# Modulation sums taken as rows in four column tiles, with a small turn in the next body, in place of four products with the sums stationary

## What is computed

```python
mod = c_act @ mod_w[i] + mod_b[i]
sh1, sc1, g1, sh2, sc2, g2, sh3, sc3, g3 = jnp.split(mod, 3 * N_SUB, axis=-1)
h = modulate(rmsnorm(x, norm_g[i, 0]), sh1, sc1)
x = x + FFN_RES * g1[:, None, :] * swiglu(h, ffn_w13[i, 0], ffn_w2[i, 0])
```

## Time and profile before

| | us |
|---|---|
| median of 3 runs | 1813.01 |
| lowest and highest run | 1812.73, 1813.53 |
| span of the profiled execution | 1812.3 |
| PE busy | 1725.8 (95%) |
| DVE busy | 1234.9 (68%) |
| ACT busy | 901.6 (50%) |
| L354 matmuls with 64 columns, 256 records | 32.4 |

### The profile page before, as it was taken

The page is one execution under the profiler, slowest core; times in us unless marked ns, Lnnn a source line. Parts: engine busy times, 40 slices in busy tenths (PEclk is TensorE's granted clock), DMA queues, the critical chain, the costliest instruction groups (busy, mean ns, idle before and its releaser), DMA issues.

```text
span 1812.3 us, 33012 instructions
## 1 busy us (share of the span) xinstructions
PE 1725.8 (95%) x12130; PEld 1582.9 (87%) x12130; DVE 1234.9 (68%) x2056; ACT 901.6 (50%) x1475; POOL 74.9 (4%) x119
## 2 busy tenths in 40 slices
PE   6999999899999999999999999999999999999998
PEld 5899989888999889998778999899877789889997
DVE  6877878668777877766556555689687465455554
ACT  2444457644444434445665444545377755554443
POOL 2000011200000100000001000100000000000000
PEclk9999999999999999999999999999999999999999
DMA  9898857758888698864434655354532155436551
GB/s 352 301 308 296 288 141 203 158 209 265 304 291 289 166 345 284 297 183 138 128 83 114 216 187 189 107 177 149 158 99 71 48 186 170 133 122 196 183 185 67
DMA packets 123657, 352.78 MB, mean 195 GB/s; under 512 B 9850, under 2 KB 52874, under 8 KB 114224
## 3 DMA queue, kind: packets, MB, share of 16 engines
q1 hardware_dynamic: 108128, 262.18, 45.4%
q10 hardware_dynamic: 12432, 78.65, 12.7%
q0 software_dynamic: 3008, 10.74, 1.8%
HBM read 347.31 MB, written 4.22 MB: 194 GB/s over the span
## 4 chain that ended last, share of the span: by engine, by line
PE 78%; DVE 11%; ACT 5%; issue 3%; DMA 1%; POOL 1%; ACTq 0%; DVEq 0%; POOLq 0%
PE ps L779 68%; DVE w_lo L189 2%; DVE arena L344 2%; ACT w_hi L183 1%; PE ps L2978 1%; PE ps L354 1%; PE ps L3064 1%; DVE resid L1205 1%; DVE arena L2671 1%; DMA arena<-in_mod_w 1%; PE ps L647 1%; PE ps L3042 1%; DMA cst<-in_const 1%; DVE tmp L344 0%; DVE tmp L1202 0%
## 5 line engine op out<-in xcount | busy, mean ns | idle before, releaser
L779 PE MATMUL ps<-t_hi,w_hi 128*128 128x256 f32 (+1 forms) x2616 | 749.4, 286 | 12.5 <-DVE t_lo L708 5.4
L779 PE MATMUL ps<-t_lo,w_hi 128*128 128x256 f32 (+1 forms) x2616 | 741.7, 284 | 0.0
L779 PE MATMUL ps<-t_hi,w_lo 128*128 128x256 f32 (+1 forms) x2616 | 741.6, 283 | 0.0
L779 PEld LDWEIGHTS ps<-t_hi,w_hi 128*128 128x128 f32 (+1 forms) x2616 | 501.1, 192 | 28.7 <-issue 14.6
L779 PEld LDWEIGHTS ps<-t_lo,w_hi 128*128 128x128 f32 (+1 forms) x2616 | 501.5, 192 | 2.1
L779 PEld LDWEIGHTS ps<-t_hi,w_lo 128*128 128x128 f32 (+1 forms) x2616 | 501.4, 192 | 0.2
L1066 DVE TENSOR_TENSOR w_lo<-raw,w_hi 128x1024 fp32r<-128x1024 f32 x258 | 313.8, 1224 | 157.6 <-ACT w_hi L1055 157.5
L189 DVE TENSOR_TENSOR w_lo<-raw,w_hi 128x1024 fp32r<-128x1024 f32 x240 | 289.1, 1224 | 129.5 <-ACT w_hi L183 129.4
L1055 ACT ACTIVATE w_hi<-raw 128x1024 fp32r<-128x1024 f32 x258 | 269.4, 1054 | 175.2 <-PE ps L779 174.7
L183 ACT ACTIVATE w_hi<-raw 128x1024 fp32r<-128x1024 f32 x240 | 248.6, 1053 | 150.9 <-PE ps L779 108.3
L779 PE MATMUL ps<-w_hi,g_hi 128*128 128x512 f32 x440 | 176.1, 400 | 6.1 <-DVE g_lo L1097 5.8
(11 more groups left out here) (349 smaller groups left out, 1662.9 us busy)
## 6 DMA issues: line engine op xcount, KB each, us to landing
raw<-in_stream SPq DMA_DIRECT2D x498, 512.0 KB, 4.3
arena<-in_mod_w ACTq DMA_DIRECT2D x72, 1024.0 KB, 6.9
grow<-gate_scratch POOLq DMA_DIRECT2D x6, 512.0 KB, 8.7
u_scratch<-u_keep ACTq DMA_DIRECT2D x1, 3072.0 KB, 34.0
arena<-u_scratch POOLq DMA_DIRECT2D x8, 256.0 KB, 3.3
small<-in_small POOLq DMA_DIRECT2D x1, 1368.0 KB, 11.5
resid<-in_x POOLq DMA_DIRECT2D x1, 1024.0 KB, 18.5
arena<-in_mem POOLq DMA_DIRECT2D x1, 1024.0 KB, 5.4
```

The lines of the kernel that those rows point to most:

```text
L779: last = TE.matmul(out, lhs, rhs, start=start and i == 0, stop=stop and i == 2)
```

## The change

For the chunks 4 to 35 the work of `mod_turn` is split in three:

- `mod_sums` on PE: 32 columns of ones are the stationary operand, and the four 128x128 pieces of `modp` move, one after the other into the four column tiles of the array (`tile_position` (0, 0), (0, 32), (0, 64), (0, 96)). The sums lie as rows in `ps[7]`, 32 equal rows for each piece. It stands where `mod_turn` stood.
- `mod_keep` on ACT: one copy of 128x128 from `ps[7]` to the new tile `mod_row`. In a body it stands between the high parts j = 4 and 5 (behind j = 5 in the first body of a call).
- `mod_turn` on PE: one matmul with `mod_row` stationary and four columns of the identity moving (columns 0, 32, 64, 96), which gives the four columns. It stands in the next body, behind the product with j = 0; in a norm right behind `mod_keep`.

`mod_add` waits for that turn and reads four adjacent columns. In the bodies it moves from between the low parts j = 4 and 5 to the next body, between modulation products 0 and 1 and the low part j = 0. `first_turn`, for chunks 0 to 3, is what it was. The last chunk of call 2 is turned in a body that has no chunk of its own.

```diff
--- before.py
+++ after.py
@@ -121,6 +121,7 @@
         posi = sb("posi", [P, QT], I32)
         u_keep = sb("u_keep", [16, 384])
         gcol = sb("gcol", [P, KT])
+        mod_row = sb("mod_row", [P, P])
         AW = 16464
         arena = sb("arena", [P, AW])
         ps = [ctx.enter_context(nc.psum_tensor(f"ps{i}", [P, 512], F32)) for i in range(8)]
@@ -163,7 +164,8 @@
         gated, gate_hi, gate_lo = sem("hidden_gated"), sem("hidden_hi_done"), sem("hidden_lo_done")
         silu_done = sem("silu_done")
         gate_stored, row_landed = sem("gate_line_stored"), sem("gate_row_landed")
-        mod_cols, mod_added = sem("mod_columns"), sem("mod_added")
+        mod_cols, mod_added = sem("mod_sums_in_rows"), sem("mod_added")
+        mod_kept, mod_turned = sem("mod_rows_kept"), sem("mod_rows_turned")
         inputs, later, scratch, stored = Count("inputs_landed"), Count("rows_landed"), Count("scratch_stored"), Count("output_stored")
         biasld, first_in = Count("bias_landed"), Count("columns_and_constants_landed")
         small_in, x_in, onehot_in = Count("small_weights_landed"), Count("x_landed"), Count("onehots_landed")
@@ -344,23 +346,36 @@
                     VE.scalar_tensor_tensor(out=total, in0=w, scalar=cact[:, k:k + 1], in1=total,
                                               op0=ALU.mult, op1=ALU.add).then_inc(mod_step, 1)
 
-        def mod_turn(pe, c, first=False, place=0):
+        def first_turn(pe, c):
             pe.wait_ge(mod_step, c * 8 + 8)
-            if not first:
-                pe.wait_ge(mod_added, c)
-            total = modp_first[c] if first else modp
             for j in range(4):
-                at, wide = (32 * (4 * c + j), 32) if first else (place + 64 * j, 64)
-                last = TE.matmul(ps[7][:, at:at + wide], total[:, j * P:(j + 1) * P], cs("ones", 0, wide), start=True, stop=True)
+                last = TE.matmul(ps[7][:, 32 * (4 * c + j):32 * (4 * c + j) + 32], modp_first[c][:, j * P:(j + 1) * P], cs("ones", 0, 32),
+                                 start=True, stop=True)
             last.then_inc(mod_cols, 1)
 
+        def mod_sums(pe, c, place=0):
+            pe.wait_ge(mod_step, c * 8 + 8)
+            pe.wait_ge(mod_added, c)
+            for j in range(4):
+                last = TE.matmul(ps[7][32 * j:32 * j + 32, place:place + P], cs("ones", 0, 32), modp[:, j * P:(j + 1) * P],
+                                 start=True, stop=True, tile_position=(0, 32 * j))
+            last.then_inc(mod_cols, 1)
+
+        def mod_keep(act, c, place=0):
+            act.wait_ge(mod_cols, c + 1)
+            E.activation(mod_row[:, :], ps[7][:, place:place + P], ACT.Copy).then_inc(mod_kept, 1)
+
+        def mod_turn(pe, c, place=0):
+            pe.wait_ge(mod_kept, c - PRE + 1)
+            TE.matmul(ps[7][:, place + P:place + P + 4], mod_row[:, :], cs("ident", 0, 97)[:, 0:97:32],
+                      start=True, stop=True).then_inc(mod_turned, 1)
+
         def mod_add(dve, c, place=0):
-            dve.wait_ge(mod_cols, c + 1)
+            dve.wait_ge(mod_turned, c - PRE + 1)
             sl = slice(c * 4, c * 4 + 4) if isinstance(c, int) else bass.ds(c * 4, 4)
             bl = slice(COL["mod_b"][0] + c * 4, COL["mod_b"][0] + c * 4 + 4) if isinstance(c, int) \
                 else bass.ds(c * 4 + COL["mod_b"][0], 4)
-            sums = ps[7][:, place:place + 256].rearrange("p (a b) -> p a b", b=64)[:, :, 0]
-            VE.tensor_tensor(modc[:, sl], sums, cols[:, bl], ALU.add).then_inc(mod_added, 1)
+            VE.tensor_tensor(modc[:, sl], ps[7][:, place + P:place + P + 4], cols[:, bl], ALU.add).then_inc(mod_added, 1)
 
         @block.scalar
         def _(act):
...
@@ -715,6 +730,14 @@
                     @block.tensor
                     def _(pe):
                         pe.wait_ge(V.sem, added[QT - 1, 1])
+                        mod_sums(pe, late_mod, place=L)
+
+                    @block.scalar
+                    def _(act):
+                        mod_keep(act, late_mod, place=L)
+
+                    @block.tensor
+                    def _(pe):
                         mod_turn(pe, late_mod, place=L)
 
                     @block.vector
@@ -976,7 +999,7 @@
             def slot(j):
                 return (h0 + j) % RING
 
-            def pe_body(pe, i, first, last_body, mod):
+            def pe_body(pe, i, first, last_body, mod, owes):
                 split = KT // 2 if first and fresh else 0
                 for k in range(split):
                     pe.wait_ge(V.sem, kt_ready[k][0])
@@ -1006,6 +1029,8 @@
                             last = triple(ps[4 + t][:, which * L:(which + 1) * L], t_hi[:, k, :], t_lo[:, k, :],
                                           wh[:, k, :], wl[:, k, :], True, k == 0, k == KT - 1)
                         last.then_inc(used, 1)
+                        if owes is not None and j == 0:
+                            mod_turn(pe, owes)
                 if last_body:
 
                     for q in range(QT):
@@ -1023,9 +1048,6 @@
                             elif t == 1:
                                 last.then_inc(T.sem, T.up())
                                 acc_step[q, f] = T.n
-                        if q == 0:
-                            if mod is not None and not late_mod and not first:
-                                mod_turn(pe, mod)
                     return
                 for t in range(2):
                     j = 4 + t
@@ -1040,7 +1062,7 @@
                                           first and t == 0, last_body and t == 1)
                     last.then_inc(used, 1)
                     if t == (1 if first else 0) and mod is not None:
-                        mod_turn(pe, mod)
+                        mod_sums(pe, mod)
 
             def hi_next(act, i, j, static):
                 h = h0 + j + RING
@@ -1067,6 +1089,7 @@
                                  ALU.subtract).then_inc(lo_done, 1)
 
             def act_body(act, i, static, mod, more):
+                late = static and i == FG - 1
                 for t in range(2):
                     hi_next(act, i, 2 * t, static)
                     act.wait_ge(used, h0 + 2 * t + 2 + RING * i)
@@ -1076,15 +1099,21 @@
                     hi_next(act, i, 2 * t + 1, static)
                     if mod is not None and more:
                         mod_load(act, t, mod + 1)
-                if not (static and i == FG - 1):
+                if not late:
                     hi_next(act, i, 4, static)
+                    if mod is not None and not (static and i == 0):
+                        mod_keep(act, mod)
                     hi_next(act, i, 5, static)
-
-            def dve_body(dve, i, static, mod):
+                    if mod is not None and static and i == 0:
+                        mod_keep(act, mod)
+
+            def dve_body(dve, i, static, mod, owes):
                 opening = static and i == 0
                 for t in range(2):
                     if mod is not None and not opening:
                         mod_products(dve, mod, range(4 * t, 4 * t + 2))
+                    if owes is not None and t == 0:
+                        mod_add(dve, owes)
                     if not (opening and t == 1):
                         lo_next(dve, i, 2 * t, static)
                     gate_first = t == 1 and static and i == FG - 1
@@ -1109,12 +1138,16 @@
                 late = static and i == FG - 1
                 if not late:
                     lo_next(dve, i, 4, static)
-                if mod is not None and not (late and late_mod):
-                    mod_add(dve, mod)
                 if not late:
                     lo_next(dve, i, 5, static)
 
-            def emit(lo, hi, mod_of):
+            def owed_of(i):
+                return i + mod0 - 1
...
@@ -1155,17 +1188,17 @@
                 blocks["hi"] = h0 + RING
                 emit(0, 1, with_mod)
                 if n_mod == FG:
-                    emit(1, FG - 1, with_mod)
+                    emit(1, FG - 1, with_mod, owed_of)
                     if residual is not None:
                         gate_row(residual)
-                    emit(FG - 1, FG, with_mod)
+                    emit(FG - 1, FG, with_mod, owed_of)
                 else:
-                    emit(1, n_mod - 1, with_mod)
-                    emit(n_mod - 1, n_mod, with_mod)
+                    emit(1, n_mod - 1, with_mod, owed_of)
+                    emit(n_mod - 1, n_mod, with_mod, owed_of)
                     for i in range(n_mod, FG):
                         if i == FG - 1 and residual is not None:
                             gate_row(residual)
-                        emit(i, i + 1, no_mod)
+                        emit(i, i + 1, no_mod, owed_of if i == n_mod else owes_none)
             else:
                 emit(0, 1, no_mod)
                 emit(1, FG - 1, no_mod)
```

19 lines of the change are left out of this document (11 added, 8 removed).

## The result

The changed kernel takes 1815.42 us (median of 20 runs, lowest 1810.82) against 1812.43 for the kernel before in the same comparison (1807.94 to 1815.17): a ratio of 1.0019, 95% interval 1.0012 to 1.0026. One of the 20 runs took 1900.86 us, at a mean granted clock of 0.851 of full speed against 0.992 to 0.997 in the others, and is left out of the ratio. Both programs were run again later: 1816.19 against 1812.77, ratio 1.0016 (1.0006 to 1.0026), and the kernel before against itself 1.0002 (0.9992 to 1.0012). So it is slower by a little under 0.2%: within the bound of "no change", but more than the forecast's 1.6 us, which would be 1.0009. The profiled execution has a span of 1814.0 (before 1812.3).

What follows compares the result with a forecast made beforehand. The prediction took a ring of PE's j = 5 and j = 0, then ACT and DVE, to set the body. Bodies 0, body 9 of call 2 0.25, norms 1.35: 1.6 us more, from 1813.0 to 1814.6; range 1811.5 to 1818.0.

Steps and rivals of the forecast that it cites:

- steps 1 and 6: 26 loop bodies: sums cost PE 0.70 us instead of 0.84; first bodies: nothing, a few hundredths either way.
- The ring through DVE: Loop body: PE's j = 5 and j = 0, then ACT and DVE for about 12 us; set 18.03 us.
- PE's margin: In each loop body PE is ready some 0.18 us too early for the gate.
- my lower end of 0.19: Lowest spread taken for the starts of the sums' eight records, in us, if four tiles halve the spacing again.
- The rival's gain: By the skill's 4 ns per tile, the rival that the wait isn't the gate's would gain more than up to 2 us.
- Steps 2 to 5: Bodies: turn 0.25 us on PE, silu delayed without harm; mod_add moved, 0.15 on DVE; mod_keep 0.3 on ACT; all cost nothing.
- Step 7: Body 9 of call 2, where PE is the bound: the turn costs its full 0.25 us (0.21 to 0.42).
- Step 8: Three late chunks in the norms: 0.45 us more each (0.25 to 0.65), 1.35 for three (0.75 to 1.95).
- PE as the bound: Loop bodies: PE needs 1.20 us a body, j = 5 starts 0.18 late in 26 bodies, total 1819.5; chance 0.16.
- the wait isn't the gate's: Loop bodies: PE's saving comes through, 0.04 to 0.07 us a body, up to 2 us, or 1809 total; chance 0.08.
- the four tiles run in a row: Sums in 26 bodies: tiles run one after another at full length, 1.26 us for the sums, 1827 total; chance 0.02.

Runs made afterwards that it cites:

- the quarter: Kernel before with one of the four modulation products in bodies and late chunks: 1814.06 us, ratio 1.0020, period 18.03.
- the longer ring: Kernel before with one idle DVE instruction ahead of the gate's multiply of t = 1 in each body: 1817.52 us, ratio 1.0037, period 18.23.
- the seven products: Kernel before with seven modulation products in place of four in the loop bodies: 1828.23 us, period 18.60.
- after_row_later: Changed kernel with GpSimd's gate row in calls 0 and 1 put behind the low part of j = 4 in body 2: 1812.64 us, ratio 1.0002.

## Why the prediction came out as it did

The time was within the range and the sign of the difference as forecast, but two of the terms that made it up were not in the working.

**The bound, and steps 1 and 6: right.** The ring through DVE holds the body, shown by the quarter (no change), the longer ring (all of its 0.20 arrives) and the seven products. PE's margin was mis-sized: 0.10, not 0.18. It didn't matter, as PE's cost fell. The eight starts spread over 0.154, less than my lower end of 0.19, and the sums cost 0.56 in an unstalled stream, where I gave 0.59 to 0.78 and took 0.70. The first body of call 1 gave back 0.13 (20.32 to 20.19 from its gate to the next body's), that of call 0 nothing (20.54, 20.53).

**The tiles, once more.** The first record starts 0.32 behind the last matmul of j = 4 (118.61, 118.93), where a step is 0.23. The Trainium skill's rule that a change of tiling mode drains TensorE ("TensorEngine Tiling (Array Packing)", Tiling Modes, Key Properties) agrees. My way to the bounds was wrong, though: I took a mean of 0.055 between the records of two tiles and asked whether four tiles halve it. The starts aren't evenly spread. In that group too the two tiles of a pass start 7 ns apart, and some 0.10 to 0.15 lies between the passes:

```profile
340.61:340.64 0.03, 0.03 (x2) 1.00 0.20 51
340.64:340.75 0.11, 0.11 (x2) 1.00 1.14 275
340.77:340.80 0.03, 0.03 (x4) 1.00 0.66 273
```

Four tiles of 32 need two passes where two tiles of 64 need four, so the waits between passes shrink from three to one. The Trainium skill ("TensorE: Matmul & The Clock Gate", Part 3, Measured speedup vs the span model) gives about 4 ns for each more tile; the trace has 6 to 7 ns within a pass, which is near it, and the spread did come out below my 0.19 as that rule said. The rival's gain didn't come with it, since PE's time was not what held the body.

**Steps 2 to 5: right in the bodies.** The turn costs 0.22 (0.25 taken) and delays no one; `mod_add` fits, and the idle time shrank by only 0.07, not 0.15: it starts (107.98) while the record of the product ahead of it still runs (107.32 + 0.75 = 108.07), and ends 0.06 behind that. `mod_keep` takes 0.26 (0.3 taken). The sentence "It has no transfer behind it that it could hold up" is true of the bodies and false of two norms, as the row at 612.84 shows.

**Step 7: right.** Body 9 of call 2 goes from 16.45 to 16.66, 0.21 for 0.25.

**Step 8: right way, size off.** 0.29 a norm, 0.87 for three, where I took 1.35. The working had 0.65 for the sums, 0.04 and 0.30 for the copy: 0.99 until it ends. It ends 253.52 - 252.74 = 0.78 behind the start of the sums, which start 0.08 later than `L354` did: 0.86. The term that was too large is the spread of the records, 0.15 and not 0.19 to 0.39. The way from there to `mod_add` was given as 0.48 and took 0.47. Together 1.33 against 1.04 before, which is the 0.29.

**What was missing.** (1) I followed `mod_add` to those who wait for it on PE and DVE, but not to GpSimd, whose row of the gate hangs on `mod_added` too and carries a transfer of 512 KB. The waits that go with it are 0 to 1.7 us a run; after_row_later shows that the row delays the weights, in one trace. (2) I gave the granted clock no term. The runs of the changed kernel have some 0.6 us worth less of it, by the estimate above, and four traces of five show the longer low stretch at the start of call 2, whose cause stays open. The 3.0 us between the medians would then be 1.1 from steps 7 and 8, about 0.9 from the row (the mean above) and about 0.6 from the clock, 2.6 in all. The compared medians have an interval of 1.3 us to either side, so that sum is no proof.

So the size was partly luck. Of my 1.6 us 1.1 came, since the norms cost 0.48 less than I took, and the rest of what was measured is from terms that I didn't have. My base of 1813.0, from three runs, also stood 0.6 above the 1812.43 measured beside the change, and that hid some of the miss. The time of 1815.42 lies at the edge of the 1814.0 to 1815.4 that the terms allowed, and well within a range that was made wide for rivals that did not come.

**The rivals.** PE as the bound did not come. That the wait isn't the gate's is refuted by the longer ring. That the four tiles run in a row is refuted by 0.43 us for eight records.

**Left open.** Why the runs of one kernel have a lower granted clock than those of another (the quarter's above all), and what makes the low stretch at the start of call 2 3.4 or 6.8 us long.

## What to carry to other kernels

An engine at 95% can still be a follower: look at what ends last ahead of its longest run of work, and at the start of the load behind it. When a cheaper step buys only idle time, shorten the ring that holds the body in the same edit, and count what the moved step then adds to that ring; here the saving on PE was worth nothing alone and 5 us together with one DVE product moved. Where differences of 0.2% are asked for, put the granted clock of the runs beside their times. When a step that others wait for is moved, list every engine that waits on its semaphore, and the transfers that those waits release.

## What the runs showed of the hardware that was not expected

Four column tiles of 32, two float32 records of 128 columns each, start 6 to 7 ns apart within a pass and 0.113 us from pass to pass, and last 0.43 together; between 512- and 256-column matmuls they cost 0.56, some 0.09 of it on entry. A matmul of 128x4 (two records) costs 0.22 in a stream of 256-column ones. The granted clock fell to 0.50 for 6.8 us in four of five traces where PE had only the short sums between two stops, and for 3.4 us in the fifth, in the kernel with a quarter of the products and in both traces of before. A run's time goes with its mean granted clock, about 1.1 us for each 0.001, and a single low stretch of 3.4 us behind call 2 costs up to 1.5. The same transfer of modulation weights lands 5.8 to 6.6 us after its issue without the gate's row beside it, 11.1 to 12.5 in before with it, and 12.1 to 14.5 with the bodies as changed, where the row's fetch starts 8.2 to 10.4 us behind the issue and not 4.7 to 5.8.
